# A hybrid decoder step on one core: the samples' input rows of the first mixer loop go through a scratch in HBM instead of eight products per head

## What is computed

```python
def _hgrn_chunk(S, inp):          # samples: L = 1
    q, logf, k, i = inp
    ...
    kd = jnp.exp(b[:, -1:] - b) * k
    S_new = jnp.exp(b[:, -1])[..., None] * S + jnp.einsum('bshc,bshv->bhcv', kd, i)
    return S_new, o
```

## Time and profile before

| what | value |
|---|---|
| runs, median (lowest to highest) | 1837.44 us (1830.11 to 1847.13) |
| profiled execution, span from its first to its last instruction | 1834.7 us |
| PE busy | 1751.2 us, 95% |
| PE weight loads busy | 1529.5 us, 83% |
| DVE busy | 1053.9 us, 57% |
| ACT busy | 790.0 us, 43% |
| POOL busy | 67.1 us, 4% |
| granted PE clock, mean over the span | 0.983 of full |
| DMA, mean | 214 GB/s |

### The profile page before, as it was taken

How to read it: one execution, slowest core, us unless ns; L and a number is a source line. 1 busy time by engine, 2 the same in 40 slices (tenths; PEclk the granted TensorE clock), 3 DMA queues, 4 the chain that set the end, 5 groups by cost and what they waited for, 6 DMA issues and landing times. The chain is left out here.

```text
span 1834.7 us, 33767 instructions
## 1 busy us (share of the span) xinstructions
PE 1751.2 (95%) x12916; PEld 1529.5 (83%) x12916; DVE 1053.9 (57%) x1903; ACT 790.0 (43%) x1428; POOL 67.1 (4%) x99
## 2 busy tenths in 40 slices
PE   5999999999999999999989999999999999989998
PEld 3898978878876787999979889778878767879997
DVE  3555555566567666565455554465565666666653
ACT  2554444345333205555345454344345222255652
POOL 0000000000001000000000000100000000000000
PEclk8999999999999999999999999999999999999999
DMA  8778565536448825555657784564553597355551
GB/s 333 265 274 335 193 222 222 200 140 243 159 162 272 317 94 190 184 179 207 252 201 269 278 318 174 222 236 161 189 194 139 189 325 255 116 196 180 181 216 61
DMA packets 85949, 391.86 MB, mean 214 GB/s; under 512 B 12472, under 2 KB 17856, under 8 KB 55488
## 3 DMA queue, kind: packets, MB, share of 16 engines
q1 hardware_dynamic: 72664, 368.15, 55.2%
q10 hardware_dynamic: 13160, 22.02, 3.4%
HBM read 377.31 MB, written 12.83 MB: 213 GB/s over the span
## 5 line engine op out<-in xcount | busy, mean ns | idle before, releaser
L1100 DVE TENSOR_TENSOR ring_parts<-ring,pages_parts 128x1024 fp32r<-128x1024 f32 (+1 forms) x288 | 334.0, 1193 | 161.8 <-ACT pages_parts L1716 161.7
L567 PE MATMUL ps<-arena_parts,pages_parts 128*128 128x264 f32 x1536 | 395.1, 291 | 18.7 <-DVE xn_parts L1188 9.8
L1716 ACT ACTIVATE pages_parts<-ring 128x1024 fp32r<-128x1024 f32 (+1 forms) x288 | 285.3, 1028 | 182.3 <-DMA ring<-in_w_ffn_in 58.6
L568 PE MATMUL ps<-xn_parts,pages_parts 128*128 128x264 f32 x1408 | 357.5, 288 | 0.0
L567 PEld LDWEIGHTS ps<-arena_parts,pages_parts 128*128 128x128 f32 x1536 | 295.2, 192 | 37.1 <-issue 31.3
L568 PEld LDWEIGHTS ps<-xn_parts,pages_parts 128*128 128x128 f32 x1408 | 269.3, 191 | 0.0
L572 PE MATMUL ps<-arena_parts,ring_parts 128*128 128x264 f32 x1536 | 222.9, 285 | 0.0
L528 PE MATMUL ps<-xn,ring 128*128 128x264 f32 x896 | 208.9, 389 | 0.6 <-ACT xn L1723 0.6
L572 PEld LDWEIGHTS ps<-arena_parts,ring_parts 128*128 128x128 f32 x1536 | 202.4, 190 | 0.0
L528 PEld LDWEIGHTS ps<-xn,ring 128*128 128x128 f32 x896 | 166.2, 190 | 34.9 <-ACT gates L1830 3.5
L567 PE MATMUL ps<-big_parts,pages_parts 128*128 128x264 f32 x704 | 176.1, 285 | 0.0
(11 more groups left out here) (351 smaller groups left out, 2592.8 us busy)
## 6 DMA issues: line engine op xcount, KB each, us to landing
ring<-in_w_ffn_in SPq DMA_DIRECT2D x88, 1024.0 KB, 5.1
ring<-in_w_ada SPq DMA_DIRECT2D x32, 1536.0 KB, 6.9
ring<-in_w_a SPq DMA_DIRECT2D x32, 1536.0 KB, 7.7
ring<-in_w_ffn_down SPq DMA_DIRECT2D x32, 1408.0 KB, 6.1
pages<-in_k_pages SPq DMA_DIRECT2D x128, 256.0 KB, 5.6
pages<-in_v_pages SPq DMA_DIRECT2D x128, 256.0 KB, 3.9
ring<-in_w_ada SPq DMA_DIRECT2D x24, 1024.0 KB, 6.6
ring<-in_w_proj SPq DMA_DIRECT2D x8, 1536.0 KB, 9.0
```

What stands on the lines that cost most here:

```text
L567: mm(ps[:, b, 0:T], tile, hi[:, k, :], start=start, stop=False)
L568: return mm(ps[:, b, 0:T], tile, lo[:, k, :], start=False, stop=False)
L1100: v.tensor_tensor(ring_lo[:, r, at * P:(at + n) * P], w, whi[:, place, 0:n * P].bitcast(F32), ALU.subtract)\
L1716: A(whi[:, place, 0:n * P], ring[:, r, at * P:(at + n) * P], ACT.Copy).then_inc(S.whi_ready, 1)
```

## The change

The eight products of `sample_rows` go from the first loop. In their place ACT stores the 128 x 8 block of columns to a scratch tensor in HBM, behind its three other stores, and later loads the block's 1024 numbers into every partition of `arena[:, 0:1024]`. In memory the block is ordered v first, then sample ("k b"), so that DVE reads a row of one sample with a step of eight elements (32 bytes). The load waits for the fourth count of `lvl` of the round (levels 0 to 3 are then read) and for the store. DVE's multiplication waits for the load, and works in place in SBUF instead of from PSUM. Two semaphores are added; `ibr` is counted in the second loop only. POOL's and SP's programs stay as they are.

```diff
+        row_store = nc.dram_tensor("sample_rows", [DEPTH, HEADS, P, NB], F32, kind="Internal").ap()
+        rows_in = part(0, NB * P)
+        hrows = rows_in.rearrange("p (k b) -> p b k", b=NB)
...
                     pe.wait_ge(S.lvc, i * 5 + 5 + since(S.lvc))
                     pe.wait_ge(S.kdtr, i + 1 + since(S.kdtr))
-                    sample_rows(M1, pj[:, HI_, TP:T]).then_inc(S.ibr, 1)
                     mm(ps[:, M0, 0:TP], vi[:, 2, :], sct[:, 0:2, :], start=True, stop=False)
...
-                    dve.wait_ge(S.ibr, i + 1 + since(S.ibr))
-                    dve.wait_ge(S.klr, i + 1 + since(S.klr))
-                    link(v.tensor_tensor(tt8, ps[:, M1:M1 + 2, :].rearrange("p a (b k) -> p (a b) k", k=P),
-                                         w4[:, TP:T].unsqueeze(2).broadcast_to([P, NB, P]), ALU.mult))
+                    dve.wait_ge(S.row_in, 16 * (i + 1) + since(S.row_in))
+                    link(v.tensor_tensor(hrows, hrows, w4[:, TP:T].unsqueeze(2).broadcast_to([P, NB, P]), ALU.mult))
                     dve.wait_ge(S.snm, i + 1 + since(S.snm))
-                    v.tensor_tensor(sn8[:], sn8[:], tt8, ALU.add).then_inc(S.snr, 1)
+                    v.tensor_tensor(sn8[:], sn8[:], hrows, ALU.add).then_inc(S.snr, 1)
...
-                    dve.wait_ge(S.ibr, HEADS + i + 1 + since(S.ibr))
+                    dve.wait_ge(S.ibr, i + 1 + since(S.ibr))
...
                     act.dma_start(outs.conv_p[layer, i], xp[:, TP:TP + 3]).then_inc(S.store, 16)
+                    act.dma_start(row_store[layer, i], pj[:, HI_, TP:T]).then_inc(S.row_out, 16)
                     softplus_tail(w1, pj[:, HF_, :]).then_inc(S.l1r, 1)
...
                             split_halves(w_slot, A_ORDER[0][n] * KC)
+                    act.wait_ge(S.lvl, i * 5 + 4 + since(S.lvl))
+                    act.wait_ge(S.row_out, 16 * (i + 1) + since(S.row_out))
+                    act.dma_start(rows_in, row_store[layer, i].rearrange("k b -> (k b)").partition_broadcast(P))\
+                        .then_inc(S.row_in, 16)
                     act.wait_ge(S.ho, i + 1 + since(S.ho))
```

More of the change, by code:

```diff
@@ L69 @@
     ss_ready=3, slot_done0=60, slot_done1=45, slot_done2=58, slot_done3=69, ada_tr=9, whi_done=192, yss_ready=3, tr=8,
-    zz=4, suf=4, av=4, qkv_ps=4, gt=5, page_free0=8, page_free1=8, page_free2=8, page_free3=8, lvl=20, kdtp=4, ibr=8,
+    zz=4, suf=4, av=4, qkv_ps=4, gt=5, page_free0=8, page_free1=8, page_free2=8, page_free3=8, lvl=20, kdtp=4, ibr=4,
     ho=4, hos=4, ztr=4, hss=8, gcp=1, sufs=1, kqr=4, value_free0=8, ndr=4, cst=4, value_free1=8, qbr=4, vrd=9, dns=4,
@@ L79 @@
     low_ready=4, sig=8, cev=4, c_out=144, cs_out=64, rsb=4, pre_pool=1, pool_it=4, x_fin=18, sqc=4, pchain=4, qstr=4,
-    snm=4, cnp=4, y_out=0, n_out=0, pre_ln=0,
+    snm=4, cnp=4, row_out=64, row_in=64, y_out=0, n_out=0, pre_ln=0,
 )
@@ L327, in build @@
             "low_ready rows_k rows_q x_own c_out cs_out obs "
-            "c_in x_in k_in t_in pre_pool pre_exp sqd pre_sum pre_link pre_dve ada_bias y_out "
+            "row_out row_in c_in x_in k_in t_in pre_pool pre_exp sqd pre_sum pre_link pre_dve ada_bias y_out "
         )
```

## The result

The changed kernel took 1861.49 us, the median of four runs (1859.19 to 1865.23), against 1837.68 for the kernel before in the same comparison: 1.0118 times as long, 95% interval 1.0085 to 1.015. It is slower by 1.2%, where 0.4% faster was forecast. The profiled execution took 1859.19 us, and its span is 22.7 us longer than that of before.

A forecast was written before the change was run, and what follows sets the result against it. PE was taken as the bound, busy 1751.2 of 1834.7 us. Removed products 15.0, less store 3.8, pages 2.4 and DVE waits 1.0, gave 7.8 us off 1837.4: 1829.6 us, 0.4% faster; 8 in 10 range 1820 to 1847.

The forecast's parts named there:

- The 15.0 us of the removed products: On PE, eight products a round take 1.88 us; over eight rounds 15.0 us, the most the change can give.
- The store's 3.8 us: ACT's new store delays the softplus and PE's suffix sums by 0.48 us in eight rounds: 3.8 us back.
- The pages: The load's 512 KB delay PE's key pages by 0.8 us in three rounds: 2.4 us, bounds 0 and 7.
- by these rows the step is free, and I take 1.23 us each: DVE's multiplication and addition, stepping by 32 bytes through `arena`, take 1.23 us each; upper bound 2.30.
- a stated doubt: On DVE's step: no row reads SBUF with such a step, and eight elements are few.
- 0.25 was put down for four: PE waits 0.25 us for DVE's new state in the four rounds where DVE had no idle time: 1.0 us.
- The first rival: The 32-byte step doubles the element time of both DVE instructions: 10.0 us more, 1839.6 us in all; chance 0.20.
- I take 3.5: ACT's new broadcast load into `arena` lands in 3.5 us, leaving 1.8 us of cover; open ends 3.2 and 13.2 us.
- the second rival: The broadcast load lands late, all descriptors reading the same 4 KB: 1846 us at 8.1, 1886 at 13.2; chance 0.16.
- The rule on row pitch: For the load: copies whose rows lie at large powers of two in HBM fell to about half their rate.
- the cover here is used up by the gain itself: At PE's new-state products: any DVE time beyond today's is paid in full in the four rounds without slack.
- 0.07 to a result over 1% slower: Whole kernel over 1856 us, by a load landing beyond some 9 us: chance 0.07.

The follow-up runs named there:

- The kernel with the repairs: The changed kernel with rows contiguous in SBUF, `w_b` held until the last broadcast load landed, and the store behind the first softplus: 0.995 of the kernel before.
- Experiment 6: The kernel before, with DVE's multiplication repeated five times in each layer's last round: 1.0102 of the kernel before; in the first round instead: 1.0092.
- the hold of `w_b`: The changed kernel, with SP issuing `w_b` only after the layer's last broadcast load has landed: 1.0007 of the kernel before.
- experiment 1: The changed kernel with the scratch laid out sample first, so that DVE steps by one element: 1.0029 of the kernel before.
- experiment 4: The changed kernel with 16 unused products on PE ahead of its new-state wait in each layer's last round: 1.006 of the kernel before.

## Why the prediction was wrong

Its list of what would be paid was right: DVE's time, the load, ACT's store, the pages. Two of the sizes were wrong, and one cost wasn't on the list. The account by waits below is read from one profile of each kernel.

- The 15.0 us of the removed products held as an upper bound. The kernel with the repairs shows that they can be had in good part: 0.5%, some 9 us, against the 12 expected of it.
- The store's 3.8 us held: PE's wait ahead of the suffix sums grew by 14.7 - 10.2 = 4.5 us, by the steps named, and moving the store took it away.
- The pages were put at 2.4 us and cost 0.7 in the profile, which is within what this wait varies by.
- The step that failed first is "by these rows the step is free, and I take 1.23 us each". It is 2.01: 1.81 ns an element in place of 1.04. Two rows with 8 and 32 elements carried it, one of them in PSUM, against a stated doubt and against the Trainium skill. Its rule on lines of 16 bytes (Advanced Engine Details and Errata, Memory Cachelines) is borne out by this trace in kind; it gives no size. PE waited in all six early rounds, 1.2 us in the mean, where 0.25 was put down for four: some 7 of the 16.5 us. The first rival had the mechanism right, its price of the step a third too high (1.07 us an instruction for 0.78) and its total too low (10.0 us; the rows contiguous gave 16 to 18 back). The row of eight elements couldn't have told: at 1.81 ns it would take 172 ns, against 167 and the 168 read.
- The second failure is in the sum for the load. "I take 3.5" was read in round one and used for all eight. In six rounds the load landed in time. In the last round of each layer showed full engines, and I used that row for the pages and not for the load itself. It landed after 9.4 us, and PE waited 4.3 and 4.9 us. That is the second rival's late load, in two rounds in place of five, and not by its repeated row: the same load landed in 3.4 to 4.8 us in every round once `w_b` was held. The rule on row pitch that this rival quotes is on rows that lie apart in memory; here all partitions read one row, so that it says nothing of this load. The Trainium skill (DMA: Bandwidth & Descriptors, Issuing engines are not separate DMA queues) says that loads of all issuing engines share the same 16 and interleave; 9.4 us with `w_b` in the queue and at most 4.8 without agree with it.
- The third is missing from the sum altogether: what a wait costs beyond itself. By waits alone the change is -15.0 + 4.5 + 16.5 + 0.7 = 6.7 us slower. The span grew by 22.7. The other 16 us are what is left over, and the clock can hold them: its mean fell from 0.983 to 0.971, which is some 22 us of full clock over the span, part of it in waits. Experiment 6 shows by itself that a wait costs about twice its length, 9.2 us for 17 to 19. The repairs agree: the rows contiguous took 10 us of waits away and gave 16 to 18, the hold of `w_b` also 10 and gave 20. With all three repairs the mean clock is that of before, and the sum by waits comes near the 9 us measured: the wait ahead of the suffix sums is 11.8 for 10.2, that for the pages 5.8 for 4.5, so -15.0 + 1.6 + 1.3 = -12.1 us. The kernel before shows what the clock is worth without any change: its fastest execution in these comparisons (1830.8 us) had a mean clock of 0.987, its slowest (1851.8) 0.973.
- The forecast rested on a cover used to the last 0.1 us ("the cover here is used up by the gain itself"). That sentence was right and should have set the likeliest case: every error in DVE's time or the load's had to come out on the same side. The forecast gave 0.07 to a result over 1% slower, and only for a load that lands after 9 us. That landing came, in two rounds; but with the rows contiguous (experiment 1) it left 4.8 us of PE's wait in all, so that the result isn't its doing alone.

Not tried: a load that reads 128 different rows of HBM, so whether the repeated row costs anything stays open; at 3.3 to 4.7 us in the first three rounds of each layer, in all profiles, where the state load took 3.5, there is little room for it. Nor is it shown what brings the second stretch of half clock, or the 7 us behind the last round in experiment 4, where PE had no wait. How the 16 us divide between the clock and the variation of single executions isn't shown either.

## What to carry to other kernels

When a removal is as long as the slack behind it, the neighbour that was early becomes the bound; put an error on each of its durations before you count the gain. Read the queue ahead of a new transfer in every round in which it is issued, not in the first one alone. And a layout chosen for a cheap store can make the reader slow: here the 4 KB store with contiguous pieces saved nothing, as it had 30 us, and cost DVE 1.6 us a round.

## What was not expected of the hardware

A float32 multiplication or addition of DVE over 128 x 1024 took 2.01 us when one of its streams stepped by 32 bytes in SBUF, the written one or one that is read, and also when two did (the multiplication in place); 1.22 us without. Ten waits of PE of 4.3 to 5.7 us were each followed directly by 7 to 14 us at 1.2 GHz, and adding 9.2 us of wait cost 17 to 19 us. Shorter waits, and once none, were followed by 7 us in some rounds. A store of 4 KB in 1024 pieces of 4 bytes landed in 13 to 14 us, in 128 pieces of 32 bytes in 7 to 8 us.
